# One decoder layer with a 32-expert mixture: how the first expert pair gets its rows, where LayerNorm's weights enter, and how head means are spread

## The chip, the cores and the metric

One core of one Trainium2 chip runs the whole layer as one program. The metric is device time in microseconds (us), the median of the runs shown. Engines: TensorE (PE; its weight loads are PEld), VectorE (DVE), ScalarE (ACT), GpSimd (POOL) and SyncE (SP), which here only starts DMA transfers.

## The reference, cut to what matters

288 rows of 1024 fp32 numbers (256 of a prompt, 32 of samples) go through one layer:

```python
proj = x @ w_in                     # q, k, v of two head groups, 8 heads x 64 each
o    = attention of both groups     # block-sparse (here one block) and dilated windows
o    = concat(RMSNorm_head(o_A) * gn_moba, RMSNorm_head(o_B) * gn_win)
hx   = LayerNorm(alpha * x + o @ w_out) * ln1_g + ln1_b
logits = hx @ w_router + b_router   # top 4 of 32, softmax over the four -> comb
for e in range(32):                 # f, the mixture
    gu   = hx @ w_gate_up[e] + b_gate_up[e]
    act  = min(gate, 7) * sigmoid(1.702 * min(gate, 7)) * (clip(up, -7, 7) + 1)
    f   += comb[:, e] * (act @ w_down[e] + b_down[e])
y    = LayerNorm(alpha * hx + f) * ln2_g + ln2_b
```

The outputs are y, and the new key and value rows of both groups. The expert weights are 403 MB of the 454 MB that are moved.

## The kernel before, in words

Everything is fp32, and each engine has one instruction stream written out by hand; engines wait on each other's semaphores. Rows are held in `hx` as three tiles: two of 128 prompt rows, and one of 32 sample rows (`TILES`, line 21).

**Projection and attention.** 29 slots (line 867 on PE, 1342 on ACT, 1637 on DVE), each with one projection product and whatever tables such as `SCORE`, `MIX` and `KEY` put in it. `mean_squares` (700) multiplies the squares of a pair of heads by `blk64`, so that each of 128 partitions gets its head's mean; four results of 256 columns each lie side by side in `msq`. In slot 19 `root_means` (1334) takes the roots of the first four, and `scale_out` (1594) inverts them and multiplies `outT`. `turn_samples(0)` (823) and `samp_place(0)` (1615) bring the samples' outputs in slot 20. Four other head pairs follow as two halves in slots 26 and 27.

**Output product, LayerNorm, router.** The order of tiles is samples, first, second (`ORDER`). For each tile DVE adds alpha * x (`raw_sum`, 1705), PE turns the raw sum (`turn_hx`, 896) and forms the logits from it, since ln1's weights are folded into the router; ACT normalises (`normalise`, 1383), DVE multiplies by ln1_g (`gain`, 1698), POOL adds ln1_b (`add_bias`, 642). DVE's `choose` (1743) takes the top four; `place_early` and `place_last` (920, 929) count rows per expert; `pick` is then a matrix of zeros and ones, rows by slots, 64 slots for each expert of a pair.

**Expert pairs.** Sixteen pairs. A pair's weights are 12 units of 2 MB: eight of gate_up, four of down. SP loads them into a ring of eight buffers (`load_unit`, 429; `unit_free`, 504). A unit is loaded over the one eight units before it, once PE has read that one. Unit 0 of the first pair has a buffer of its own, `first`, so the first pair's units 0 to 8 can be loaded ahead; units 9, 10, 11 of it and unit 0 of the second wait for its units 1, 2, 3, 4 to be read. PE's order for a pair is: `gather` (1026; pick times hx, 6 products), `turn_weights`, `turn_act`, `down` (1085) of the pair before with `turn_slots` (1035) of the new one in it, four bias products for each expert in `begin_gate_up` (1128), `gate_up` (1041) with `combine` of the pair before in it. The first pair instead forms its turned rows at once in `gather_first` (941), 24 products of 128 columns, and `add_biases` (1006) puts combT times b_down into the sums after unit 3. ACT copies turned rows to `xg` (1420).

Between unit 8 and units 9 on, SP has a wait of its own:

```python
        sp.wait_ge(S.hx_ready, 5)            # 495
        sp.wait_ge(S.hx_last, 1)
        sp.dma_start(ln_g[:, :], ln2_g[0:1, :].broadcast_to([128, D])).then_inc(S.ln2_in, 16)
```

Of the kernel before, what the change touches and what calls it, by code (L numbers as in the profile page):

```python
# [63 lines left out]
def constant_tables():  # L64
# [11 lines left out]
    att = np.zeros((128, A_END + 128), np.float32)  # L76
    att[:, A_END:] = (p[:, None] // HD == p[None, :] // HD) / HD
# [30 lines left out]
def build_layer(nc, x_prompt, x_sample, cache_k, cache_v, state_k, state_v, page_table, w_in, gn_moba,  # L108
# [9 lines left out]
    def place(name, shape, at=None, dt=F32):  # L118
# [44 lines left out]
    ln_gs, ln_bs = place("ln_gs", [128, 256]), place("ln_bs", [128, 256])  # L163

# [7 lines left out]
    blk64 = place("blk64", [128, 128], at=share_at + 2592)  # L172
# [7 lines left out]
    bdn = place("bdn", [E, D], at=ybuf_at)  # L180
    combT = place("combT", [E, T], at=spread_at)
# [15 lines left out]
    msq = place("msq", [128, 4, SEQ])  # L197
    upper = place("upper", [NS, 512], at=top_at + 4096)
# [10 lines left out]
        probs_copied head_mixed out_taken squared msq_done msq_taken msq_rooted outT_ready  # L209
# [3 lines left out]
        hx_ready hx_last hx_raw hx_halved hx_turned hxT_ready router_folded router_summed routed logits_read logits_used  # L213
# [5 lines left out]
        y_ready mixed added y_varied y_rooted y_scaled y_centred y_gained hx_gained y_normed y_done y_moments y_shared  # L219
        sums_whole copies_out  # L220
# [37 lines left out]
    c_folded, c_consts = columns(2 * E), columns(2 * E)  # L258
# [103 lines left out]
    def _(sp):  # L362
# [109 lines left out]
        sp.dma_start(ln_b[:, :], ln1_b[0:1, :].broadcast_to([128, D])).then_inc(S.ln1_in, 16)  # L472
# [10 lines left out]
        sp.dma_start(bdn[:, :], b_down[0]).then_inc(S.bdn_in, 16)  # L483
# [11 lines left out]
        sp.wait_ge(S.hx_ready, 5)  # L495
        sp.wait_ge(S.hx_last, 1)
        sp.dma_start(ln_g[:, :], ln2_g[0:1, :].broadcast_to([128, D])).then_inc(S.ln2_in, 16)
        sp.dma_start(ln_b[:, :], ln2_b[0:1, :].broadcast_to([128, D])).then_inc(S.ln2_in, 16)
# [28 lines left out]
        load_units(0, 0, range(9, UNITS))  # L527
        next_bias(0)
# [48 lines left out]
    def _(pool):  # L577
# [72 lines left out]
        pool.wait_ge(S.ln1_in, 32)  # L650
        for nth in range(2):
            add_bias(hx, ORDER[nth], S.hx_gained, S.hx_ready, nth)
        low = hx[:, ORDER[2], 0:512]
        pool.wait_ge(S.hx_centred, 5)
        nc.gpsimd.tensor_tensor(low, low, ln_g[:, 0:512], ALU.mult).then_inc(S.hx_halved, 1)
        pool.wait_ge(S.hx_halved, 1)
        nc.gpsimd.tensor_tensor(low, low, ln_b[:, 0:512], ALU.add).then_inc(S.hx_ready, 1)
        pool.wait_ge(S.ln2_in, 160)
# [1363 lines left out]
```

## Time and profile before

| | |
|---|---|
| median of 3 runs | 1183.83 us (1183.76 to 1184.81) |
| the profiled execution | 1188.98 us, its span 1187.1 us |
| instructions | 14412 |
| PE busy | 1141.0 us (96%) |
| DVE, ACT, POOL busy | 297.0, 175.3, 38.4 us |
| moved by DMA | 454.45 MB, mean 383 GB/s |
| mean granted clock of TensorE | 0.986 |

The span is the time from the first to the last instruction of the execution that was profiled. Times in the rows are microseconds from its start. A granted clock of 1.00 is 2.4 GHz, 0.50 is 1.2 GHz. In a line such as `144.36 0.41 PE L665 MATMUL ... x2 [3.38 <-DVE otS L1613]` the first number is the start, the second the time that the group takes, and the bracket is the idle time of the engine before it and what ended it. Matmuls overlap, so a busy PE need not be at its peak. A product of fp32 operands is two matmul instructions.

### The profile page before, as it was taken

To read this page: it belongs to the slowest core of one execution; us is meant where nothing else is said; L and a number is where in the kernel's file an instruction comes from. 1 tells how busy PE (TensorE), PEld (TensorE's weight loads), DVE (VectorE), ACT (ScalarE), POOL (GpSimd) and SP (SyncE) were. 2 spreads that over 40 slices of the span, in tenths; PEclk is the share of its full clock that TensorE was granted. 3 is DMA by queue.
4 is the path that set the end of the run, shared out by engine and by line. 5 is a ranking of instruction groups with operands and counts; after the bars stand their busy time and mean duration, and the time that the engine had idled before them with its cause. 6 is when DMAs were issued, how large, how long until landed. Compare 5 with 4: busy or idle time off the path is not lost.

```text
span 1187.1 us, 14412 instructions
## 1 busy us (share of the span) xinstructions
PE 1141.0 (96%) x5520; PEld 469.3 (40%) x5521; DVE 297.0 (25%) x702; ACT 175.3 (15%) x381; POOL 38.4 (3%) x71
## 2 busy tenths in 40 slices
PE   8999889999999999999999999999999999999996
PEld 6877654553333333333333333333333333333332
DVE  1453756822021212121211203030303030303113
ACT  1332322211010101010202010101010111111111
POOL 0110111200000000000000000000000000000001
PEclk9999999889999999999999999999999999999998
DMA  9957749758999999999999999999999999999993
GB/s 350 320 195 255 266 176 413 305 199 344 407 427 426 428 428 427 428 428 428 428 428 428 428 428 428 428 427 428 428 428 428 428 428 427 428 428 428 413 422 123
DMA packets 83397, 454.45 MB, mean 383 GB/s; under 512 B 7146, under 2 KB 20098, under 8 KB 36130
## 3 DMA queue, kind: packets, MB, share of 16 engines
q1 hardware_dynamic: 81008, 441.49, 90.2%
q0 software_dynamic: 1728, 10.75, 2.4%
q10 hardware_dynamic: 626, 1.75, 0.4%
q8 instruction: 21, 0.34, 0.1%
q14 instruction: 14, 0.11, 0.0%
HBM read 450.43 MB, written 11.93 MB: 389 GB/s over the span
## 4 chain that ended last, share of the span: by engine, by line
PE 75%; DMA 18%; DVE 4%; ACT 2%; SPq 1%; issue 1%; DVEq 0%
PE bank L1055 23%; PE bank L1097 18%; DMA ring<-in_w_gate_up 16%; PE bank L1031 8%; PE bank L688 6%; PE bank L665 5%; PE bank L1122 3%; PE bank L835 2%; PE bank L691 2%; DMA ring<-in_w_down 2%; PE bank L1206 1%; PE bank L790 1%; PE bank L1138 1%; PE bank L956 1%; SPq L448 1%; ACT actT L1286 1%
## 5 line engine op out<-in xcount | busy, mean ns | idle before, releaser
L1055 PE MATMUL bank<-ring,xg 128*64 128x512 f32 x1904 | 420.6, 598 | 10.6 <-DMA ring<-in_w_gate_up 10.6
L1055 PEld LDWEIGHTS bank<-ring,xg 128*64 128x64 f32 x1904 | 133.6, 137 | 288.9 <-issue 263.6
L1097 PE MATMUL bank<-ring,actT 128*64 128x512 f32 x960 | 215.9, 597 | 3.8 <-ACT actT L1286 3.8
L1888 DVE TENSOR_TENSOR acc<-acc,bank 128x512 f32<-128x512 f32 x60 | 41.2, 687 | 493.6 <-PE bank L1122 493.6
L1097 PEld LDWEIGHTS bank<-ring,actT 128*64 128x64 f32 x960 | 66.6, 137 | 121.5 <-issue 118.7
L1429 ACT ACTIVATE sig<-gate 128x256 f32<-128x256 f32 x64 | 26.7, 417 | 528.0 <-DVE gate L1870 528.0
L1031 PE MATMUL bank<-hx,pick 128*128 128x512 f32 x180 | 90.0, 625 | 0.0
L1870 DVE TENSOR_SCALAR gate<-bank 128x256 f32<-128x256 f32 x64 | 26.9, 420 | 186.7 <-PE bank L1055 166.5
L688 PE MATMUL bank<-xT,wblk 128*128 128x288 f32 x256 | 68.4, 423 | 0.9 <-DVE xT L1517 0.9
L1122 PE MATMUL bank<-ybuf,spread 128*128 128x512 f32 x120 | 58.4, 618 | 0.0
L688 PEld LDWEIGHTS bank<-xT,wblk 128*128 128x128 f32 x256 | 49.4, 198 | 16.4 <-issue 2.4
L1031 PEld LDWEIGHTS bank<-hx,pick 128*128 128x128 f32 x180 | 29.1, 187 | 60.7 <-issue 60.7
L1286 ACT ACTIVATE xg<-bank 128x512 f32<-128x512 f32 x32 | 19.1, 597 | 126.2 <-PE bank L665 112.0
L835 PE MATMUL bank<-wout,outT 128*128 128x512 f32 (+1 forms) x96 | 36.6, 600 | 0.4 <-ACT kstage L1286 0.4
L1122 PEld LDWEIGHTS bank<-ybuf,spread 128*128 128x128 f32 x120 | 19.1, 188 | 39.0 <-DVE acc L1888 19.7
L648 POOL TENSOR_TENSOR acc<-acc,ln_b 128x512 f32<-128x512 f32 x2 | 3.0, 1510 | 945.7 <-DVE acc L1981 945.7
L1286 ACT ACTIVATE ybuf<-bank 128x512 f32<-128x512 f32 x31 | 16.9, 594 | 108.5 <-PE bank L1097 96.5
L691 PE MATMUL bank<-wblk,xT 128*128 128x256 f32 x128 | 30.1, 390 | 0.0
L1176 PE MATMUL bank<-ring,xg 128*64 128x512 f32 x128 | 28.6, 596 | 0.9 <-DMA ring<-in_w_gate_up 0.8
L1874 DVE SCALAR_TENSOR_TENSOR up<-up,gate 128x256 f32<-128x256 f32 x64 | 27.2, 425 | 2.7
L1871 DVE TENSOR_SCALAR up<-bank 128x256 f32<-128x256 f32 x64 | 26.6, 416 | 0.0
L691 PEld LDWEIGHTS bank<-wblk,xT 128*128 128x128 f32 x128 | 24.6, 197 | 3.4 <-issue 0.2
(236 smaller groups left out, 724.1 us busy)
## 6 DMA issues: line engine op xcount, KB each, us to landing
ring<-in_w_gate_up SPq DMA_DIRECT2D x119, 2048.0 KB, 25.4
ring<-in_w_down SPq DMA_DIRECT2D x63, 2048.0 KB, 27.2
ring<-in_w_gate_up SPq DMA_DIRECT2D x16, 1024.0 KB, 18.7
wblk<-in_w_in SPq DMA_DIRECT2D x12, 1024.0 KB, 8.0
kring<-in_cache_k_moba SPq DMA_DIRECT2D x16, 256.0 KB, 5.0
vring<-in_cache_v_moba SPq DMA_DIRECT2D x16, 256.0 KB, 5.1
out<-in_state_k_win POOLq DMA_DIRECT2D x8, 512.0 KB, 4.8
out<-in_state_v_win POOLq DMA_DIRECT2D x8, 512.0 KB, 5.8
```

Of the source, the lines that this page charges most:

```text
L665: return nc.tensor.transpose(out, in_, ident[0:in_.shape[0], 0:in_.shape[0]])
L688: ins = nc.tensor.matmul(out[:, 0:T], w[:, k, 128 * c:128 * c + 128], xT[:, k, :], start=(k == 0), stop=(k == KC - 1))
L691: ins = nc.tensor.matmul(out[:, 0:256], xT[:, k, 128 * c:128 * c + 128], w[:, k, :], start=(k == 0), stop=(k == KC - 1))
L835: return nc.tensor.matmul(out_bank(t, half), outT[:, k, t0:t0 + rows], wout[:, k, 512 * half:512 * half + 512], start=(k == 0), stop=(k == ...
L1031: ins = nc.tensor.matmul(bank[6 + a][:, :], pick[0:rows, t, :], hx[0:rows, t, 512 * a:512 * a + 512], start=(t == 0), stop=(t == 2))
L1055: ins = nc.tensor.matmul(bank[n][64 * e:64 * e + 64, :], xg[:, k, 64 * e:64 * e + 64], w[:, 2048 * e + 512 * n:2048 * e + 512 * n + 512], ...
L1097: ins = nc.tensor.matmul(bank[4 + half][64 * e:64 * e + 64, :], actT[:, j, 64 * e:64 * e + 64], w[:, at:at + 512], start=(j == 0), stop=(j ...
L1122: ins = nc.tensor.matmul(bank[4 + half][:, :], spread[:, t0:t0 + rows], ybuf[:, 512 * half:512 * half + 512], start=True, stop=True)
L1176: ins = nc.tensor.matmul(bank[n][64 * e:64 * e + 64, :], xg[:, k, 64 * e:64 * e + 64], w[:, at:at + 512], start=False, stop=(k == KC - 1))
L1286: return nc.scalar.activation(out, in_, ACT.Copy, **kw)
L1874: V.scalar_tensor_tensor(up[:, c], up[:, c], 1.0, gate[:, c], ALU.add, ALU.mult).then_inc(S.dve_moe, 1)
L1888: V.tensor_tensor(o, o, new, ALU.add).then_inc(S.added, 1)
```

## The change

- The copy of a normalised row no longer has ln1_g and ln1_b in `hx`. They enter where turned rows are copied to `xg`: eight ACT instructions with a scale and a bias for each partition in place of two copies. The sums get alpha * ln1_g * hx from DVE (`scale_sums`), and alpha * ln1_b as a 33rd row of b_down against a row of alpha in combT. POOL's work on `hx`, and DVE's `gain` and `last_half`, are gone.
- The first pair is gathered like the others: pick times hx tile by tile, copied to `xtok`, turned, copied to `xg`.
- The samples' part of every gather is two 32-row parts of the array, one for each half of the columns; for this the samples' second half is copied to partitions 32 to 63 (`lower_half`), and `posm` too.
- Bias products of a pair: four with 128 columns of weights in place of eight with 64.
- Of the first four head pairs the means lie in 32 partitions each of one 256-column tile; they are inverted at once, and PE spreads them (`spread_means`) before DVE scales. The samples' turn of group 0 moves from slot 20 to 24, to another bank.
- `add_biases` is split in three parts, after units 4, 5 and 6 of the first pair; `keep_warm(1)` is one product whose result is not used; ln2_b is loaded where ln1_b was; ln2_g is loaded after `scale_sums`, between units of the ring.

```diff
+        def spread_means(pair):
+            pe.wait_ge(S.msq_inverted, 1)
+            pe.wait_ge(S.outT_ready, pair)
+            for c in range(2):
+                j = 2 * pair + c
+                ins = nc.tensor.matmul(bank[4][:, 256 * c:256 * c + 256], heads_of[:, 128 * j:128 * j + 128], msq[:, 0, :],
+                                       start=True, stop=True)
+            ins.then_inc(S.means_spread, 1)
...
-            if slot in (20, 27):
-                turn_samples(0 if slot == 20 else 1)
+            if slot in (20, 21):
+                spread_means(slot - 20)
+            if slot in (24, 27):
+                turn_samples(0 if slot == 24 else 1)
...
+        def invert_means():
+            dve.wait_ge(S.msq_rooted, 1)
+            V.reciprocal(msq[:, 0, :], msq[:, 0, :]).then_inc(S.msq_inverted, 1)
+
+        def scale_pair(pair):
+            dve.wait_ge(S.means_spread, pair + 1)
+            o = outT[:, 2 * pair:2 * pair + 2, 0:SEQ]
+            V.tensor_tensor(o, o, bank[4][:, :].rearrange("p (c q) -> p c q", c=2), ALU.mult).then_inc(S.outT_ready, 1)
...
             if slot == 19:
                 samp_squares(0)
-                scale_out(0, 0, 4)
+                invert_means()
                 samp_norm(0)
-            if slot == 20:
+            if slot in (20, 21):
+                scale_pair(slot - 20)
+            if slot == 24:
                 samp_place(0)
...
+        def gather_samples():
+            for a in range(2):
+                r = slice(NS * a, NS * a + NS)
+                nc.tensor.matmul(bank[6 + a][:, :], pick[r, 2, :], hx[r, 2, 512 * a:512 * a + 512], start=True, stop=False,
+                                 tile_position=(NS * a, 0))
+
+        def gather_tile(t, a):
+            return nc.tensor.matmul(bank[6 + a][:, :], pick[:, t, :], hx[:, t, 512 * a:512 * a + 512], start=False,
+                                    stop=(t == 1))
+
+        def gather_first():
+            pe.wait_ge(S.first_picked, 1)
+            pe.wait_ge(S.hx_low, 1)
+            gather_samples()
+            place_last()
+            pe.wait_ge(S.hx_centred, 4)
+            for a in range(2):
+                gather_tile(0, a)
+            pe.wait_ge(S.picked, 1)
+            for a in range(2):
+                pe.wait_ge(S.hx_centred, 5 + a)
+                gather_tile(1, a).then_inc(S.gathered, 1)
+
+        def keep_warm(n):
+            for _ in range(n):
+                nc.tensor.matmul(bank[0][:, :], ident, keep[:, 0:512], start=True, stop=True)
...
         turn_hx(2, 0)
         place_early()
+        keep_warm(1)
         turn_hx(2, 1)
...
         begin_gate_up(0)
-        place_last()
-        for nth in range(3):
-            gather_first(nth)
-        gate_up(0, 0, 0, {1: turn_comb, 3: add_biases})
+        place_known()
+        gather_first()
+        turn_slots(0, 0)
+        turn_slots(0, 1)
+        gate_up(0, 0, 0, {1: turn_comb, 4: lambda: add_biases(0), 5: lambda: add_biases(1), 6: add_sample_biases})
...
-                for e in range(2):
-                    ins = nc.tensor.matmul(bank[n][64 * e:64 * e + 64, :],
-                                           keep[r, C_SEL + SLOTS * e:C_SEL + SLOTS * (e + 1)],
-                                           bias_rows[r, :], start=True, stop=False, tile_position=(32 * n, 64 * e))
+                ins = nc.tensor.matmul(bank[n][:, :], keep[r, C_SEL:C_SEL + 2 * SLOTS], bias_rows[r, :], start=True,
+                                       stop=False, tile_position=(32 * n, 0))
...
-                copy(xg[:, 4 * a:4 * a + 4, :], bank[7 - a][:, :].rearrange("p (k s) -> p k s", k=4)).then_inc(S.xg_ready, 1)
+                for k in range(4 * a, 4 * a + 4):
+                    ins = nc.scalar.activation(xg[:, k, :], bank[7 - a][:, 128 * (k % 4):128 * (k % 4) + 128], ACT.Identity,
+                                               bias=s_(c_cols + KC + k), scale=s_(c_cols + k))
+                ins.then_inc(S.xg_ready, 1)
...
         load_units(0, 0, range(9, UNITS))
+        sp.wait_ge(S.sums_scaled, 6)
+        sp.dma_start(ln_g[:, :], ln2_g[0:1, :].broadcast_to([128, D])).then_inc(S.ln2_in, 16)
         next_bias(0)
```

## Rows read from the trace of the kernel before

**Rows 1.** The page: GB/s in 40 equal slices of the span.
```profile
GB/s 350 320 195 255 266 176 413 305 199 344 407 427 426 428 428 427 428 428 428 428 428 428 428 428 428 428 427 428 428 428 428 428 428 427 428 428 428 413 422 123
```
**Rows 2.** The chain that ended last: gathers of two early and two late pairs.
```profile
340.37 5.95 PE bank L1031 x12
...
397.15 5.95 PE bank L1031 x12
...
854.27 5.94 PE bank L1031 x12
...
877.92 31.79 DMA ring<-in_w_gate_up
...
913.41 5.94 PE bank L1031 x12
```
**Rows 3.** Stages: busy PE, PEld, DVE, ACT, POOL; granted clock; DMA share; GB/s.
```profile
255.00:310.00 55.00, 54.65 (x241) 18.32 (x239) 9.95 (x23) 7.93 (x15) 0.00 (x0) 0.94 0.90 360
360.00:1100.00 740.00, 724.13 (x3269) 245.54 (x3267) 128.84 (x299) 84.45 (x167) 0.00 (x0) 1.00 1.01 428
```
**Rows 4.** Timeline: PE's first pair, and SP's issues for the ring.
```profile
247.08 3.65 PE L1055 MATMUL bank<-first,xg 128*64 128x512 f32 x16 [0.69 <-ACT xg L1286]
...
254.21 7.84 SPq L438 DMA_DIRECT2D ring<-in_w_down  x3
...
273.44 34.14 SPq L438 DMA_DIRECT2D ring<-in_w_gate_up  x8
...
295.33 0.66 PE L665 MATMUL bank<-keep,xtok 128*128 128x128 f32 x4
```
**Rows 5.** Timeline of DVE, then of PE, in slots 19 to 21.
```profile
136.09 6.55 DVE L1597 RECIPROCAL msq<-msq 128x1024 f32<-128x1024 f32 x1 [1.28 <-ACT msq L1336]
142.68 1.23 DVE L1598 TENSOR_TENSOR outT<-outT,msq 128x1024 f32<-128x1024 f32 x1
...
149.64 0.95 DVE L1621 COPY outT<-bank 64x64 f32<-64x64 f32 x4
...
144.36 0.41 PE L665 MATMUL bank<-keep,otS 128*64 128x128 f32 x2 [3.38 <-DVE otS L1613]
144.60 3.62 PE L691 MATMUL bank<-wblk,xT 128*128 128x256 f32 x16
...
148.93 0.66 PE L665 MATMUL bank<-keep,kring 128*128 128x128 f32 x4 [0.27 <-DVE kT L1560]
152.77 0.55 PE L665 MATMUL bank<-keep,sampP 128*128 128x128 f32 x3 [3.19 <-DVE sampP L1566]
```
**Rows 6.** Stages as in rows 3, with PE at the lower clock.
```profile
153.00:157.00 4.00, 4.00 (x16) 3.49 (x15) 1.21 (x3) 1.02 (x3) 0.00 (x0) 0.57 0.00 0
...
229.00:245.00 16.00, 16.00 (x82) 13.78 (x83) 5.85 (x23) 2.17 (x4) 2.53 (x2) 0.50 0.70 262
...
266.00:272.00 6.00, 6.00 (x24) 1.56 (x18) 1.02 (x3) 0.00 (x0) 0.00 (x0) 0.50 0.86 362
```
**Rows 7.** Timeline of PE from the logits of the first tile on.
```profile
218.63 1.87 PE L914 MATMUL bank<-wrt,outT 128*128 128x32 f32 x16
...
227.07 0.40 PE L925 MATMUL bank<-mask,keep 32*128 32x32 f32 x2 [2.63 <-DVE mask L1757]
...
228.72 3.46 PE L914 MATMUL bank<-wrt,outT 128*128 128x32 f32 x16
232.11 2.01 PE L1138 MATMUL bank<-bias_rows,keep 2*64 2x512 f32 x16
...
236.33 10.06 PE L956 MATMUL bank<-pick,hx 32*128 32x128 f32 x48
...
307.10 1.11 PE L1138 MATMUL bank<-bias_rows,keep 2*64 2x512 f32 x16
```
**Rows 8.** POOL's second addition, and one DVE line: min/median/max ns of three.
```profile
223.40 2.87 POOL L648 TENSOR_TENSOR hx<-hx,ln_b 128x512 f32<-128x512 f32 x2 [3.91 <-DVE hx L1703]
...
L1754 DVE CAST small<-idx_u x3: 172/1020/1031, 218.5 to 233.8; 128x8 f32<-128x8 uint32 x3
```

More of the change, by code:

```diff
@@ L494, in _ @@
             load_unit(0, 0, u)
[L495 to L498, printed above, removed]
+        sp.wait_ge(S.hx_raw, 2)
         for q in range(4):
@@ L936, in place_last @@
                 nc.tensor.matmul(at, ones[:, 0:rows], first_tile, start=False, stop=False)
+        def place_last():
+            out = bank[5]
             pe.wait_ge(S.masks_ready, 3)
@@ L1004, in turn_comb, with add_biases, add_sample_biases @@
             ins.then_inc(S.comb_turned, 1)
-        def add_biases():
-            pe.wait_ge(S.combT_ready, 1)
-            pe.wait_ge(S.bdn_in, 16)
-            for j in range(4):
-                t, half = divmod(j, 2)
-                t0, rows = TILES[t]
-                if j >= 2:
-                    pe.wait_ge(S.added, j - 1)
-                nc.tensor.matmul(bank[4 + half][0:rows, :], combT[:, t0:t0 + rows],
+        def add_biases(t):
+            t0 = TILES[t][0]
+            for half in range(2):
+                if t == 0 and half == 0:
+                    pe.wait_ge(S.combT_ready, 1)
+                    pe.wait_ge(S.bdn_in, 32)
+                if t == 1:
+                    pe.wait_ge(S.added, half + 1)
+                nc.tensor.matmul(bank[4 + half][:, :], combT[:, t0:t0 + 128],
                                  bdn[:, 512 * half:512 * half + 512], start=True, stop=True).then_inc(S.spread_down, 1)
+        def add_sample_biases():
             pe.wait_ge(S.added, 3)
+            pe.wait_ge(S.sums_scaled, 2)
             for q in range(4):
                 r, c = slice(NS * q, NS * q + NS), slice(256 * q, 256 * q + 256)
-                nc.tensor.matmul(bank[4][r, 0:256], ident[0:NS, 0:NS], hx[0:NS, 2, c], start=True, stop=True,
+                nc.tensor.matmul(bank[4][r, 0:256], ident[0:NS, 0:NS], samp_x[:, c], start=True, stop=True,
                                  tile_position=(0, NS * q))
@@ L1028, in gather @@
             pe.wait_ge(S.actT_ready, turned_before)
+            gather_samples()
             for a in range(2):
-                for t, (t0, rows) in enumerate(TILES):
-                    ins = nc.tensor.matmul(bank[6 + a][:, :], pick[0:rows, t, :], hx[0:rows, t, 512 * a:512 * a + 512],
-                                           start=(t == 0), stop=(t == 2))
-                ins.then_inc(S.gathered, 1)
+                gather_tile(0, a)
+                gather_tile(1, a).then_inc(S.gathered, 1)
         def turn_slots(i, a):
@@ L1832, in _ @@
         moments(2, 0)
-        gain(hx, ORDER[1], 1, S.hx_centred, S.hx_gained)
+        lower_half()
         choose(1)
@@ L1904, in _ @@
         weigh_slots(0, 0)
+        scale_sums()
         pick_slots(1, 1, 0)
```

155 lines of the change are left out of this document (71 added, 84 removed).

## Prediction

> **What bounds the kernel now.** I read the page's DMA line first. The reader is to see that from about 300 us on the transfers run at 427 or 428 GB/s to the end, and that the holes lie before that [rows 1]. The stage of 740 us says it with a share: 1.01 at 428 GB/s, and PE busy beside it [rows 3]. So both look full; the chain tells which counts. An early pair takes 397.15 - 340.37 = 56.8 us from gather to gather, on PE; a late pair 913.41 - 854.27 = 59.1 us, and half of that is a wait for gate_up weights [rows 2]. PE is the faster one by 2.3 us a pair and runs into the transfers at last. The ring is then refilled without a hole, so the end is this: the moment when the stream of weights starts for good, plus the bytes left over 428 GB/s, plus a tail that the change leaves alone. What PE saves inside a pair of the loop is worth nothing; what lets the stream start earlier, or fills a hole in it, is worth all of it.
>
> The stream starts when PE has read unit 1 of the first pair: PE begins at 247.08, SP issues at 254.21 [rows 4], 7.1 us later. Then a hole: units 9, 10, 11 go out, and the next waits for unit 4, which comes after add_biases: 273.44 [rows 4]. In 255 to 310 the rate is 360 GB/s [rows 3]: 55 x (1 - 360/428) = 8.7 us of transfer are missing, 0.5 of it the lag of the first issue, so 8.2 us of hole.
>
> Three things to work out, then: how much earlier PE begins the first pair (A, B), how much of the hole goes (C), and what is new in the transfers (D). The sum is made in the profiled execution (1188.98 us, span 1187.1), and the difference is taken off the median, 1183.83, which is 5.2 us (0.4%) below it.
>
> **A. Head means and the samples' turn.** DVE inverts 1024 columns in 6.55 us and multiplies in 1.23; PE stands 3.38 us for the samples behind it, 0.27 for a copy and 3.19 for the probabilities sampP, in all 6.84 us [rows 5]. In 153 to 157 the granted clock is then 0.57 [rows 6]: 4 x 0.43 = 1.7 us more. After: 256 columns, 6.55/4 = 1.64 us; the multiplication and the samples' copies (0.95) move behind. DVE reaches sampP earlier by 4.9 + 1.2 + 0.95, less a scaling of about 0.7 (half of 1.23 and PSUM's read), some 6.4 us: 152.7 becomes 146.3. PE without waits gets there at 152.77 - 6.84 + 0.9 = 146.8. So DVE is just in time; what is late next is PE's own row of projections. PE gains two times four products of 256 columns at 3.62/16 = 0.23 us: 1.8 us. A = -6.84 - 1.7 + 1.8 = -6.7. If half of the waits return as another wait of the same slots, and the clock falls after it all the same, A = -1.6. Behind it transfers stood still (0 GB/s in 153 to 157 [rows 6]), so all loads up to unit 8 can move with PE.
>
> **B. From the router to the first pair.** PE waits 2.63 us for the second tile's mask [rows 7]. DVE's chain to it loses two multiplications by ln1_g (1.3 us each in other rows of that form) and the delays beside POOL: the cast takes 1020 ns in the median where the third took 172, and POOL's additions lie over both of the long casts (one of them shown) [rows 8]. That is over 3 us in each of two chains, so the 2.63 go. keep_warm adds 2 products of 512 columns, 0.9 us.
> From 227 on nearly all of PE's work ran at clock 0.50 [rows 6]: logits 3.46 against 1.87 before, bias products 2.01 against 1.11 later, the gather 10.06 [rows 7]. What is there after, at clock 1.00, from 224.45: place 0.9, keep_warm 0.9, turn 0.6, ACT's copy 0.6 and half the logits 0.9, bias 1.0, six small count products 1.2, samples 1.0, four tile products 3.5, ACT's copy 0.6, two turns 1.5, ACT's last four 128-column copies 1.0, semaphores 0.3: 14.0, the first pair at 238.4, 8.6 us earlier. (Items without a row here are read from the same timeline, halved where it ran at 0.50. 512 columns at 1.00: the loop's gather, 5.95 us for 12 [rows 2], of which the four with few rows take longer, so 0.43 for the others.) At clock 0.50 from the logits on, 8.2 us of these double: 246.6, 0.5 us earlier. So B lies between -8.6 and -0.5. I take the middle, -4.6: keep_warm stands right where the clock fell, but after it come two or three us of small products, of few rows and few columns, which is what ran when it fell before; and the full-width gather is then the sort of work in which it came back.
> Cost at nothing: lower_half (about 0.4 us of DVE), hidden by DVE's wait for the second tile's logits; scale_sums (4 products of 0.69 and two more, done about 8 us after the picks), hidden, since SP's new wait for it stands behind unit 11, 14 us after PE begins; behind that wait are the next pair's biases and all of its units. Uncovered, each us late is a us of hole. Eight ACT copies in the loop: PE asks for xg a whole half of down() later.
>
> **C. The hole.** From unit 1 read to unit 8 read PE took 295.33 - 254.21 = 41.1 us [rows 4]. Seven units of 2.097 MB at 428 GB/s are 34.3 us, and ln2_g is 1.2 us in the same stream: 35.5. PE's way gets shorter by the gather (5.95 to 4.7), by 3.0 us if the spell at 0.50 in 266 to 272 [rows 6] goes, by 0.5 for the biases' waits: 36.4, and 0.9 of hole is left; with the spell, 3.9. I take 2.3, and 0.7 for unit 9: hole 8.2 to 3.0. With ln2_g's bytes C = -5.2 + 1.2 = -4.0 (from -6.1 to -1.5).
>
> **D. New bytes.** 0.28 MB of tables at the start, where DMA is the limit: 0.65 us at 428 GB/s; half of it lies beside PE's turning: +0.3 (0 to 0.7).
>
> **The loop.** The gather loses its second small-row pass, 1.2 us a pair; bias products 0 to 0.5. PE's pair: 55.6 or less against 59.1. Worth 0 while transfers bound.
>
> Where the trace and a page could part: the four small-row products cost 5.95 - 8 x 0.43 = 2.5 us, 0.6 each, more than a full-row one. The Trainium skill (TensorEngine Tiling (Array Packing), Tiling Modes, Key Properties) says that going from one tiling of the array to another drains the engine, which speaks against 32-row parts between full tiles. By the row, the switches are paid for already and become fewer; by the page alone each pair would pay two drains, and the sum here stays as it is, since it is within PE's 3.5 us of slack.
>
> **Sum.** -6.7 - 4.6 - 4.0 + 0.3 = -15.0: span 1172.1, median 1168.8. All at their best: -6.7 - 8.6 - 6.1 = -21.4, 1162.4. All at their worst: -1.6 - 0.5 - 1.5 + 0.7 = -2.9, 1180.9.
>
> **Rivals.** (1) The clock stays low: 0.50 from the logits to well into the first pair, and again at its biases. For it: it was 0.50 through 16 us in which PE was busy all the time [rows 6], and the new order has as many small products there. Against: keep_warm, and 512 columns in place of 128. A stays, B -0.5, C -1.5, D +0.3: -8.4, 1175.4. The Trainium skill (TensorE: Matmul & The Clock Gate, Part 1) calls the low clock the default, which activity lifts; this trace agrees in that it fell behind the 2.63 us of waiting [rows 6, 7]; by the page alone the new order, without that wait, should keep the clock, as in B's better end. (2) A's waits come back as others (DVE has only 0.5 us to spare at sampP): A -1.6, the rest as forecast, -9.9, 1173.9. (3) Everything is hidden by transfers, which would need a stream that has no hole before 300 us; [rows 1] shows several: 0, 1183.8. (4) Slower: the gather's small-row parts and its turns bring the clock down inside every pair. Such a spell costs 3 us (6 us at 0.50 [rows 6]). One a pair gives 58.6 and is hidden; from two on PE passes 59.1: 61.6, 15 x 2.5 = 37.5 lost, 15 won: 1206. Against: the old gather had small-row products too, and the clock stayed at 1.00 through 740 us [rows 3]. (5) The 32-row parts do not run side by side: 0.9 us in B, nothing in the loop: 1169.7.
>
> **Chances.** Forecast with (5), -12 to -21: 0.65. (1) 0.17. (2) 0.10. (3) 0.04. (4) 0.04. The range 1161.5 to 1177.5 leaves out (3), (4) and combinations of (1) with (2). No change is within 0.2%, 2.4 us, about what a measurement of this kernel can tell: same 0.04, slower 0.04, faster 0.92.
>
> **What would show it.** A: the samples' scores of slot 20 and the second turn of slot 21 on PE with under 1 us between, no bracket at sampP, clock 1.00 through, projection of slot 22 near 149. B: no wait at the mask line; first unit near 236 (before: 247.08), 232 at clock 1.00 and 240 at 0.50. C: the rate between SP's first issue of unit 9 and 50 us later near 400 GB/s, no pause in issues after unit 11. Loop: 59.1 us a pair from the second or third pair on, PE waiting at gate_up, 428 GB/s. Wrong if a late pair is not bound by transfers, or if PE begins the first pair at the same place.

## The result, and the profile after

Measured: 1180.58 us (1178.47 to 1182.39, 15 runs), against 1185.14 (1183.76 to 1189.3) for the kernel before in the same runs, 4.6 us less by the medians. The ratio of the runs, which is not the quotient of the two medians, is 0.995, interval [0.994, 0.996], so 4.7 to 7.1 us less. The forecast was 1168.8, with a range of 1161.5 to 1177.5. The sign was right, the size wrong by 11.8 us, and the time lies outside the range. The profiled execution of after took 1180.89 us.

The page after: the rates in 40 equal slices.
```profile
GB/s 361 324 197 254 269 270 384 257 263 341 423 428 427 427 428 428 429 428 428 428 428 428 428 428 428 428 427 428 429 428 428 428 428 428 428 428 428 413 424 108
```
The span is 1178.8 us, 8.3 us shorter than in the first profile (1187.1), and the picture is that of [rows 1]: holes until about 300 us, then 427 to 429 GB/s. What has to be compared is again how early the stream of weights starts for good.

Timeline of after in slots 20 to 22 (DVE's inversion, then PE; a bracket would be idle time ahead of the row). It answers to [rows 5].
```profile
135.28 1.75 DVE L1636 RECIPROCAL msq<-msq 128x256 f32<-128x256 f32 x1 [0.64 <-ACT msq L1364]
...
141.71 3.62 PE L690 MATMUL bank<-wblk,xT 128*128 128x256 f32 x16
...
146.04 0.49 PE L664 MATMUL bank<-keep,sampP 128*128 128x128 f32 x3
...
147.89 3.62 PE L690 MATMUL bank<-wblk,xT 128*128 128x256 f32 x16
```
No bracket is left; the projection of slot 22 starts at 147.89 and takes 3.62 us, which is clock 1.00.

Timeline of PE in after, from the logits to the first pair, answering to [rows 7] and the first row of [rows 4]:
```profile
217.67 1.10 PE L987 MATMUL bank<-keep 128*128 128x512 f32 x2
...
219.04 1.93 PE L932 MATMUL bank<-wrt,outT 128*128 128x32 f32 x16
...
222.79 1.70 PE L964 MATMUL bank<-hx,pick 32*128 32x512 f32 x4
...
225.12 6.12 PE L968 MATMUL bank<-hx,pick 128*128 128x512 f32 x8
231.92 1.09 PE L664 MATMUL bank<-keep,xtok 128*128 128x128 f32 x8 [0.69 <-ACT xtok L1313]
235.57 5.35 PE L1083 MATMUL bank<-first,xg 128*64 128x512 f32 x16 [2.56 <-ACT xg L1450]
240.75 3.60 PE L1083 MATMUL bank<-ring,xg 128*64 128x512 f32 x16
```
The first pair starts at 235.57 (before 247.08). The logits ran at full speed, the four gather tiles did not (x8, since each product is two instructions): later in this trace they take 3.70 us, here 6.12. And the first unit took 5.35 us where the second took 3.60.

Stages of after: busy PE, PEld, DVE, ACT, POOL; granted clock; DMA share; GB/s. They answer to [rows 3, 6].
```profile
224.00:230.00 6.00, 6.00 (x12) 2.79 (x11) 4.32 (x17) 0.00 (x0) 0.00 (x0) 0.50 0.90 351
...
236.00:241.00 5.00, 5.00 (x18) 1.55 (x16) 0.00 (x0) 0.00 (x0) 0.00 (x0) 0.66 0.00 0
...
270.00:275.00 5.00, 5.00 (x17) 1.58 (x18) 3.06 (x8) 0.83 (x2) 0.00 (x0) 0.66 1.01 426
...
255.00:310.00 55.00, 54.50 (x229) 18.39 (x229) 10.04 (x23) 8.35 (x19) 0.00 (x0) 0.97 0.92 374
360.00:1100.00 740.00, 708.96 (x3161) 244.06 (x3159) 128.67 (x299) 107.42 (x245) 0.00 (x0) 1.00 1.01 428
```
Three spells at 0.50 (1.2 GHz) are left: some 7 us before the first pair, and two of about 3.4 us inside it. From 360 to 1100 nothing is new but PE's busy time, 15 us less.

Timeline of SP's issues for the ring in after (and PE's turn before unit 8 is free), answering to [rows 4]:
```profile
244.40 7.84 SPq L445 DMA_DIRECT2D ring<-in_w_down  x3
...
255.30 43.24 SPq L445 DMA_DIRECT2D ring<-in_w_gate_up  x8
...
286.29 0.66 PE L664 MATMUL bank<-keep,xtok 128*128 128x128 f32 x4
```
The start of the stream comes 9.8 us earlier than in the first profile. But from unit 9's issue to the freeing of unit 8 PE takes 286.29 - 244.40 = 41.9 us. It was 41.1, and 36.4 were forecast. In place of a stretch that shrinks there is one that grew a little.

Where the 5.5 us of that stretch are, the samples' bias products show. First the kernel before, the products on `hx` and on `bdn`, then the next unit (engine, line, rows*columns of the weights, the moving operand):
```profile
265.38 0.74 PE L1020 MATMUL bank<-hx,keep 32*32 32x256 f32 x8
265.84 1.13 PE L1022 MATMUL bank<-bdn,combT 32*32 32x256 f32 x8
266.90 5.39 PE L1055 MATMUL bank<-ring,xg 128*64 128x512 f32 x12
```
The same in after:
```profile
266.18 0.61 PE L1049 MATMUL bank<-samp_x,keep 32*32 32x256 f32 x2
266.73 0.62 PE L1051 MATMUL bank<-bdn,combT 33*32 33x256 f32 x2
...
270.54 2.43 PE L1083 MATMUL bank<-ring,xg 128*64 128x512 f32 x6
```
Before, all eight products take 266.90 - 265.38 = 1.5 us; after, one starts every 0.545 us, 270.54 - 266.18 = 4.4 us. The change gave `combT` and `bdn` a 33rd row (`33*32`), and it is a product of that kind that now alternates with one of 32 rows. Then the clock falls (0.66 in 270 to 275).

### The profile page after: what moved, and what is told of

It is laid out like the page before. It is cut to its first block, busy times and chain, and to the rows that moved or that the text cites. A ratio compares the mean times of both kernels' runs of the same rounds, so it can differ in the third digit from the quotient of the medians.

```text
span 1178.8 us, 14219 instructions
## 1 busy us (share of the span) xinstructions
PE 1121.9 (95%) x5374; PEld 457.7 (39%) x5375; DVE 289.7 (25%) x707; ACT 203.8 (17%) x479; POOL 30.1 (3%) x65
## 4 chain that ended last, share of the span: by engine, by line
PE 65%; DMA 26%; SPq 5%; ACT 2%; DVE 1%; issue 1%
DMA ring<-in_w_gate_up 23%; PE bank L1083 19%; PE bank L1125 15%; PE bank L968 5%; PE bank L664 5%; PE bank L687 5%; SPq L445 3%; PE bank L851 3%; PE bank L690 2%; DMA ring<-in_w_down 2%; PE bank L1150 2%; PE bank L964 1%; SPq L455 1%; PE bank L804 1%; ACT xtok L1313 1%; ACT actT L1313 1%
## 5 line engine op out<-in xcount | busy, mean ns | idle before, releaser
L1450 ACT ACTIVATE xg<-bank,small 128x128 f32<-128x128 f32 x128 | 48.1, 458 | 99.1 <-PE bank L664 99.1
L968 PE MATMUL bank<-hx,pick 128*128 128x512 f32 x128 | 61.6, 626 | 0.0
L968 PEld LDWEIGHTS bank<-hx,pick 128*128 128x128 f32 x128 | 24.0, 197 | 35.8 <-issue 35.8
L1921 DVE TENSOR_TENSOR up<-up,sig 128x256 f32<-128x256 f32 x64 | 25.3, 417 | 0.0
```

What stands on the lines that cost most here:

```text
L968: return nc.tensor.matmul(bank[6 + a][:, :], pick[:, t, :], hx[:, t, 512 * a:512 * a + 512], start=False, stop=(t == 1))
L1450: ins = nc.scalar.activation(xg[:, k, :], bank[7 - a][:, 128 * (k % 4):128 * (k % 4) + 128], ACT.Identity, bias=s_(c_cols + KC + k), scale ...
```

## The experiments

Times are medians; each ratio is against the kernel before in the same set of runs, whose own median moved from 1185.14 to 1187.27 between the sets. The four columns behind are read from one profiled execution, whose own time is given, since it can lie 3 us from the median. The last is the time from the issue of unit 9 until unit 8 is read and free.

| kernel | us | ratio to before | profiled us | first pair | unit 9 | unit 9 to unit 8 free |
|---|---|---|---|---|---|---|
| before, first profile | 1185.14 | 1 | 1188.98 | 247.08 | 254.21 | 41.1 |
| after | 1180.58 | 0.995 [0.994, 0.996] | 1180.89 | 235.57 | 244.40 | 41.9 |
| head means alone | 1181.21 | 0.9954 [0.994, 0.9967] | 1181.61 | 239.39 | 246.52 | 41.1 |
| samples' products grouped | 1174.44 | 0.9899 [0.9886, 0.9913] | 1171.77 | 232.13 | 240.75 | 37.0 |
| filling products | 1177.59 | 0.9936 [0.992, 0.9952] | 1175.3 | 233.85 | 240.97 | 40.2 |
| 3 products more a pair | 1188.2 | 1.0014 [1.0003, 1.0024] | 1189.92 | 235.52 | 244.35 | 43.5 |
| before again (one run) | 1185.87 |  | 1185.87 | 243.25 | 250.38 | 41.1 |
| grouped, filled, copy shared | 1171.95 | 0.9874 [0.9856, 0.9892] | 1172.15 | 233.44 | 240.57 | 37.0 |
| no warming product | 1179.11 | 0.9941 [0.9926, 0.9955] | 1178.33 | 233.26 | 242.08 | 41.8 |
| loop's gather as before | 1181.66 | 0.9962 [0.9949, 0.9976] | 1181.14 | 233.89 | 242.72 | 44.7 |
| samples' products, 32 rows | 1174.93 | 0.9902 [0.9882, 0.9922] | 1174.69 | 235.51 | 244.33 | 36.9 |
| as the best, no warming | 1174.15 | 0.989 [0.9868, 0.9911] | 1174.52 | 235.02 | 242.15 | 37.0 |
| grouped, copy shared | 1173.68 | 0.9883 [0.9858, 0.9909] | 1174.64 | 235.93 | 243.06 | 37.0 |

**The head means alone**, put into the kernel before; the router, the gather and the pair are as they were. In words:
```diff
-    spread head means with blk64 (128x128), 1024 columns inverted
+    means of each pair of heads in 32 partitions of one tile, 256 columns inverted, spread by heads_of after it
+    samples' turn in slot 24
```


> The kernel before with the head means alone (means in 32 partitions each, one inversion of 256 columns, PE spreads them, the samples' turn moved to slot 24). Theory (the stream's start sets the end): PE stops waiting in slots 20 and 21, reaches the first pair 6.5 to 7.5 us earlier, SP issues unit 9 as much earlier, and the hole behind it stays: 6 to 7 us less than the kernel before, ratio 0.994 to 0.995. That would be as much as the whole change gives. Rival (what is won in attention is hidden by transfers or taken by a later wait): under 2 us.

PE's timeline at the mask and the first pair, and SP's issue of unit 9, in this kernel:
```profile
219.89 0.63 PE L949 MATMUL bank<-mask,keep 32*128 32x32 f32 x2 [2.64 <-DVE mask L1797]
...
239.39 3.65 PE L1079 MATMUL bank<-first,xg 128*64 128x512 f32 x16 [0.69 <-ACT xg L1310]
...
246.52 7.84 SPq L443 DMA_DIRECT2D ring<-in_w_down  x3
```
1181.21 us: this one part wins what the whole change wins (0.9954 against 0.995, intervals over each other). It is 4.9 us less than its own kernel before (1186.09), a little under the 6 to 7 expected; the interval of the ratio, 3.9 to 7.1 us, holds them. The first pair starts 7.7 us earlier than in the first profile. The wait at the mask is still there, 2.64 us. The whole change starts the pair 3.8 us earlier still and issues unit 9 2.1 us earlier, and has nothing to show for it: something in the pair takes it back.

**The samples' products in two groups.** Same products, other order.
```diff
             for q in range(4):
                 matmul(bank[4][r, 0:256], ident, samp_x[:, c], tile_position=(0, NS * q))
+            for q in range(4):
                 matmul(bank[4][r, 256:512], combT[:, SEQ:T], bdn[:, c], tile_position=(0, NS * q))
```


> The changed kernel, the samples' eight products of add_sample_biases in another order: first the four with the 32-row identity, then the four with the 33 rows of combT, in place of turn about. Theory: turn about, each product waits for the one before (0.55 us each, 4.4 us together, where the old kernel needed 1.6); in two groups they take about 1.8 us, the stretch from unit 1 read to unit 8 read shrinks from 41.9 to about 39, and the hole in the transfers with it: 2 to 4 us less than the changed kernel (1180.6), more if the clock no longer falls in the last unit. Rival (the 4.4 us come from the 33 rows themselves, or the hole is set by something else): no change, 1180.6.

Timeline of this kernel: SP's unit 9, the samples' products on PE, the unit behind them, the turn before unit 8 is free.
```profile
240.75 7.84 SPq L445 DMA_DIRECT2D ring<-in_w_down  x3
...
262.53 0.63 PE L1049 MATMUL bank<-samp_x,keep 32*32 32x256 f32 x8
263.09 0.64 PE L1053 MATMUL bank<-bdn,combT 33*32 33x256 f32 x8
263.66 3.65 PE L1085 MATMUL bank<-ring,xg 128*64 128x512 f32 x16
...
277.71 0.66 PE L664 MATMUL bank<-keep,xtok 128*128 128x128 f32 x4
```
The eight take 263.66 - 262.53 = 1.1 us, the unit behind them runs at full clock (3.65 us, where after took 5.35), and the stretch is 277.71 - 240.75 = 37.0 us. The time falls by 6.1 us. The profiled execution, 1171.77 us, was the shortest of the five, and not all that it shows is the order: in it the gather ran at clock 1.00 and the pair began at 232.13, before the changed place is reached. So the order was tested once more in another way, below.

How far the clock in the gather differs between executions, two profiles show. Up to the end of the first gather this kernel and the one with grouped products and shared copy (last in the table) give PE the same instructions. The window 224 to 230 in this one, then in that one (the three last columns are clock, DMA share, GB/s):
```profile
224.00:230.00 6.00, 4.88 (x18) 2.38 (x18) 5.35 (x19) 2.03 (x5) 0.00 (x0) 1.00 0.84 336
...
224.00:230.00 6.00, 6.00 (x13) 2.46 (x10) 3.32 (x15) 0.00 (x0) 0.00 (x0) 0.50 0.86 340
```
Of eight traces with the same instructions there (the after kernel's and those of seven experiments), this one shows no fall of the clock before the first pair; in the others it fell between 221.7 and 224.4. In the five of them that also turn and copy as the after kernel does, the first pair begins between 232.13 and 235.57. So a difference of up to 3.4 us in the table's column for the first pair can be that of two executions and not of two kernels.

**Filling products**, one of 512 columns before the turned rows and three behind them, on a bank that is free there.
```diff
         gather_first()
+        keep_warm(1, 4)
         turn_slots(0, 0)
         turn_slots(0, 1)
+        keep_warm(3, 4)
```


> The changed kernel with one full product whose result is not used between the first pair's gather and its turns, and three after the turns, so that PE works where it stood 0.7 and 2.6 us. Theory: the clock stays at 1.00 in the first pair's first unit (it was 0.50 for 3.4 us, 1.7 us of loss), unit 9 is issued 1 to 1.7 us earlier, total 1 to 2 us less than the changed kernel. Rival (the clock falls there for another reason, or the fillers delay the first pair as much as they win): 0 to 0.5 us more.

1177.59 us; six runs from 1175.3 to 1181.26, so the interval is wide, and the profiled execution is the shortest of them. It shows the first unit at 3.65 us in place of 5.35, and unit 9 3.4 us earlier (240.97). PE no longer stands idle while ACT copies, and the spell in the first unit is gone; that is 1.7 of the 3.4 us, and the rest is there before the first filling product, in a shorter spell in the gather. The samples' eight products alternate as in after and take 267.12 - 262.76 = 4.4 us, but the unit behind them runs at full clock:
```profile
267.12 3.65 PE L1083 MATMUL bank<-ring,xg 128*64 128x512 f32 x16
```
The stretch is 40.2 us, and the hole behind unit 11 stays:
```profile
275.00:285.00 10.00, 9.50 (x49) 3.86 (x47) 0.56 (x1) 3.49 (x8) 0.00 (x0) 1.00 0.64 248
```
248 GB/s over 10 us: an earlier start does not mend C.

**Three products more in each pair of the loop** (2.6 us a pair, 14 pairs), to test the statement that PE's time in a pair is worth nothing.
```diff
-    gate_up(i + 1, ..., {3: lambda: combine(i)})
+    gate_up(i + 1, ..., {3: lambda: combine(i), 6: lambda: keep_warm(3, 7)})
```


> The changed kernel with three full products whose results are not used after unit 6 of gate_up in each of 14 pairs of the loop: 2.6 us of PE a pair, 36 us in all. Theory (from about 300 us on only transfers count, PE has 3.5 us a pair to spare): no change, within 1 us of 1180.6. Rival (PE's chain through the pairs is part of the end): up to 36 us more; half of the pairs PE-bound would give some 18.

The loop's stage in this kernel, and then the gathers of an early and of a late pair on PE's timeline:
```profile
360.00:1100.00 740.00, 733.42 (x3196) 255.07 (x3193) 128.29 (x298) 102.34 (x233) 0.00 (x0) 1.00 1.01 428
```
```profile
336.84 3.70 PE L968 MATMUL bank<-hx,pick 128*128 128x512 f32 x8
395.32 3.70 PE L968 MATMUL bank<-hx,pick 128*128 128x512 f32 x8
...
921.18 3.70 PE L968 MATMUL bank<-hx,pick 128*128 128x512 f32 x8
979.65 3.70 PE L968 MATMUL bank<-hx,pick 128*128 128x512 f32 x8
```
And in after:
```profile
332.35 3.70 PE L968 MATMUL bank<-hx,pick 128*128 128x512 f32 x8
387.90 3.70 PE L968 MATMUL bank<-hx,pick 128*128 128x512 f32 x8
...
728.24 3.70 PE L968 MATMUL bank<-hx,pick 128*128 128x512 f32 x8
787.38 3.70 PE L968 MATMUL bank<-hx,pick 128*128 128x512 f32 x8
```
7.6 us slower than after, where no change was expected, although the transfers' mean rate is 428 GB/s from 360 to 1100 in both. The added work takes PE's pair from 55.5 to 58.4 us, early and late, so PE enters the stage behind the stream and never catches up: at 921 it still goes at its own pace. In after it goes at 55.55 us until about 610 and is held by the transfers (59.14) from then on: in five or six pairs it caught up 59.14 - 55.55 = 3.6 us each, a lag of 18 to 22 us. Fifteen pairs give PE 54 us of slack, the lag takes its part, 32 to 36 are left, and 14 x 2.9 = 41 do not fit: 5 to 9 us too much, 7.6 measured. This sum is an estimate; what the traces show beside it is that behind 300 us PE waits for weights 27.1 us in all in after and not once here. "Worth nothing" holds up to a sum over the loop, not for each pair by itself.

**The kernel before once more**, unchanged, for its profile.

> The kernel before, unchanged, profiled a second time. Its first profiled execution took 1188.98 us, where the median of its other executions is 1185 to 1186. Theory (the prediction read its terms from an execution in which the clock fell at costlier places than usual): here the stretch from SP's issue of unit 9 to PE's last turn before unit 8 is read, 41.1 us in the first profile, is shorter by the 3 us of the spell at 0.50 behind add_biases, and the time is near 1185. Rival (the same spells in every execution, the 4 us are overhead of the profiler): again near 1189 with the spell at the same place.

Its logits of the first tile, its first pair, SP's unit 9, and the turn before unit 8 is free:
```profile
215.33 1.87 PE L914 MATMUL bank<-wrt,outT 128*128 128x32 f32 x16
...
243.25 3.65 PE L1055 MATMUL bank<-first,xg 128*64 128x512 f32 x16 [0.69 <-ACT xg L1286]
...
250.38 7.84 SPq L438 DMA_DIRECT2D ring<-in_w_down  x3
...
291.43 0.66 PE L665 MATMUL bank<-keep,xtok 128*128 128x128 f32 x4
```
Span 1184.1 us in place of 1187.1. The stretch is 291.43 - 250.38 = 41.05 us, the same as in the first profile, against what was expected of it. The 3 us lie ahead: the logits start at 215.33 (218.63 in [rows 7]). 1.6 us of it are there before the scores of slot 20, 1.7 come between them and those of slot 22: the wait at sampP is 0.98 us here in place of 3.19, and the clock fell ahead of it (0.63 in 143 to 150) and not behind it (1.00 in 150 to 157). The first profile was one of the longer executions (1188.98 us; the kernel's runs go from 1183.76 to 1189.3).

**Three things at once**: the grouped products, one filling product before and one behind the turned rows, and half of the first `xg` copied by VectorE beside ScalarE. Of the edit only the third is shown:
```diff
-        take_slots(0)
+        take_slots(0, (0,))                       # ACT: the first half
+        for k in range(4, KC):                    # DVE: the second
+            V.tensor_scalar(xg[:, k, :], bank[6][...], s_(c_cols + k), s_(c_cols + KC + k), mult, add)
```


> The changed kernel with three edits: the samples' bias products in two groups (e2), one filler product before and one behind the first pair's turns, and the second half of the first xg copied by DVE beside ACT. Theory (the end is the start of the stream of weights plus what hole is left): PE begins the first pair 1 to 1.5 us earlier than in e2 and at clock 1.00 more often, no hole: 2 to 3 us below e2, 1171.5 to 1172.5. Rival (with the hole gone the transfers are bound by something earlier, such as the loading of units 7 and 8): as e2, 1174.4.

The first pair on its timeline, and then the stage behind (the last column is GB/s):
```profile
233.44 3.65 PE L1085 MATMUL bank<-first,xg 128*64 128x512 f32 x16 [1.21 <-DVE xg L1954]
```
```profile
245.00:310.00 65.00, 64.50 (x293) 21.79 (x291) 13.51 (x29) 8.35 (x19) 0.00 (x0) 1.00 1.00 410
```
1171.95 us, the best of all: 0.9874 of before, 0.7% ahead of after (1171.95 / 1180.58 = 0.9927; the two were not timed in the same runs, but their ratios, 0.9874 and 0.995, say the same). Against after its unit 9 is 3.8 us earlier and its stretch 4.9 us shorter; 8.7 in all, and the span is 8.6 shorter (1170.2).

**Without the warming product** (`keep_warm(1)` between the turned rows and the last logits), all else as after.
```diff
-        keep_warm(1)
```


> The changed kernel without keep_warm(1), the one product behind the router's counting. Theory A (it keeps the clock up at least through the logits): without it the clock falls one spell earlier, as in the kernel before, and it costs 1 to 3 us. Theory B (the clock falls behind it in any case, when the small products of the counts and biases run): 0.9 us is won or nothing, 1179.7 to 1180.6.

1179.11 against 1180.58: 1.5 us less, about the product's own 0.95 us, but the intervals of the ratios lie over each other. In the profile the clock falls all the same, at about 223.5, and the first unit takes 5.35 us again. The product wins nothing here that a run shows.

**The loop's gather as before**: six full-width products a pair in place of the two-part samples and four tiles.
```diff
-            gather_samples()
             for a in range(2):
-                gather_tile(0, a)
-                gather_tile(1, a)
+                for t, (t0, rows) in enumerate(TILES):
+                    matmul(bank[6 + a], pick[0:rows, t, :], hx[0:rows, t, ...])
```


> The changed kernel with the loop's gather as before: six products, the samples' part one full-width product for each half of the columns, not two 32-row parts. Theory: PE takes 1.2 us more a pair; 14 of the 15 are hidden by PE's room, one lies in the hole before unit 8 is read: 1.2 us more, 1181.8. Rival (the row parts count in every pair): up to 18 us more. Second rival (nothing at all): 1180.6.

1181.66, 1.1 us more than after: the 1.2 us of one gather (6.00 against 1.13 + 3.70), the one of the first pair, which lies in the stretch. (In its profile the stretch is 44.7 and not 43.1, because the unit ahead of the gather ran at the lower clock for longer, 6.49 us for it against 5.35.) That the other 14 cost nothing agrees with the loop's slack. The interval [0.9949, 0.9976] lies over after's, so the size is weakly shown.

**Alternating, but of 32 rows.** The order is after's; only the 33rd row is taken from the samples' `combT` products.
```diff
-                matmul(bank[4][r, 256:512], combT[:, SEQ:T], bdn[:, c], tile_position=(0, NS * q))
+                matmul(bank[4][r, 256:512], combT[0:NS, SEQ:T], bdn[0:NS, c], tile_position=(0, NS * q))
```


> The kernel after, in which the samples' four combT products read 32 rows (combT[0:32], bdn[0:32]) in place of 33; the order (samp_x and combT products in turn) is the kernel after's own. The 33rd row of comb is left out for the 32 sample rows, so their output lacks that row's part. Theory A (the 0.55 us each is paid because a product of 33 rows and one of 32 rows put TensorE's array into different row parts, and each change waits for the product before): the eight now take 1.2 us or less in all, as the two grouped runs of four did, and the time falls by what 3.2 us earlier at that place is worth: 1177.0 to 1178.5 us. Theory B (it is the alternation itself that costs: another moving operand, the other half of the bank, the column part that repeats): they take 4.4 us as before, and the time stays at 1180.6.

SP's unit 9, the samples' products, the unit behind them, and the turn before unit 8 is free; then the window in which after's clock was 0.66:
```profile
244.33 7.84 SPq L445 DMA_DIRECT2D ring<-in_w_down  x3
...
266.12 0.65 PE L1049 MATMUL bank<-samp_x,keep 32*32 32x256 f32 x8
266.57 0.63 PE L1051 MATMUL bank<-bdn,combT 32*32 32x256 f32 x8
267.13 3.65 PE L1083 MATMUL bank<-ring,xg 128*64 128x512 f32 x16
...
281.18 0.66 PE L664 MATMUL bank<-keep,xtok 128*128 128x128 f32 x4
```
```profile
270.00:275.00 5.00, 5.00 (x16) 1.85 (x13) 4.23 (x12) 1.83 (x4) 0.00 (x0) 1.00 1.02 433
```
This is the clean comparison. Unit 9 goes out where it does in after (244.33, 244.40). The eight take 267.13 - 266.12 = 1.0 us, alternating as they do; so it is the mix of 33 and 32 rows that costs, and neither the order as such nor the bank. The spell behind them is gone too, and the stretch is 36.9 us, half a us from the 36.4 forecast. The time is 1174.93: 5.65 us less than after (5.7 by the two ratios, 0.9902 and 0.995). 3.3 us of it are the products themselves and 1.7 the spell; 0.6 stays unexplained. That was more than the 2.1 to 3.6 us expected.

Whether the spell belongs to the alternation is not shown. In four of the five traces with it the unit behind took 4.98 to 6.54 us, but with the filling products 3.65. In the five traces with the products grouped or at 32 rows the clock stays up there. But in all three traces with before's bias products, which mix no 33rd row, it falls somewhere in 257 to 272.

**The best version without the warming product.**
```diff
-        keep_warm(1)
```


> The version of e6_fast_first (samples' products in two groups, one 128x512 product on bank 4 before and after the turned slots, half of the first xg copied by VectorE) without the warming product of L987 between the turned rows and the last logits. If that product only costs (as in the kernel after without it, -1.5 us): 1170.5 to 1171.5, against 1171.95. If in this version the clock falls earlier or longer without it: 1173 or more, and the first pair starts later than 230.2 us.

1174.15, the pair at 235.02 in place of 233.44: the clock was down from 221 on, where in the version with the product it fell at 224. The first expectation was 0.5 to 1.5 us less; the time is in the second's, 1173 or more. (The 230.2 us of the expectation is no sign: it is where the turned rows begin in the version with the product, whose pair begins at 233.44.) But the early fall is not the missing product's for certain: in the next kernel, which has it, the clock fell at 221.7. And the ratios 0.989 [0.9868, 0.9911] and 0.9874 [0.9856, 0.9892] lie over each other, and the two were not timed in the same runs. Whether the product helps beside the fillers stays open.

**Grouped products and the shared copy, no filling.**

> The samples' products in two groups and half of the first xg copied by VectorE, without the two filling products. Against the grouped version alone (1174.4 us) the copy should be worth 1.0 to 1.4 us of the start (ScalarE's eight took 2.9 us, two engines with four each 1.5): 1173.0 to 1173.5. If it is the filling products that made the 2.5 us between the grouped version and the one with all three (1171.95), the time stays at 1174.4 and the clock reads 0.50 at the start of the first unit.

1173.68, 0.2 above its forecast, but the interval [0.9858, 0.9909] holds the grouped version's 0.9899. The trace shows the copy's worth: 1.46 us of waiting ahead of the first pair, where ACT alone made it 2.56. The first unit then ran at full clock, without filling products. The clock had fallen at 221.7 and stayed at 0.50 through the gather, so the pair begins at 235.93 all the same.

## Why the prediction was wrong in size

**What held.** That only the start of the stream and its holes count: in after unit 9 goes out 6.0 us earlier than in the repeated profile of before, the stretch behind it is 0.9 us longer, together -5.1, and the spans differ by -5.3 (1178.8, 1184.1). In the best version the same sum gave 8.7 for 8.6. Over all traces it reads so: from the moment when unit 8 is free to the end of the span it is 891.4 to 893.5 us in twelve of them, though that moment moves from 277.5 to 295.3. Only the kernel with three products more a pair takes longer, 900.0. What also held is the direction, and "no wait at the mask".

**A, -6.7 forecast.** From the head scores' first product of slot 20 (136.88 before, 136.71 after) to that of slot 22 the first profile of before takes 22.2 us and after 14.7: -7.4. Against the repeated profile (20.5) it is -5.8. DVE reached sampP in time, the clock kept up. A alone gave 1181.21, 4.9 us less than its own kernel before. Right.

**B, -4.6 forecast.** The first pair is 11.5 us earlier than in the first profile; without A's 7.4, -3.9 (upstream 0.2 off). The spell at 0.50 came, in the middle between B's two ends, as taken: 224 to 230 and not the logits. Right, but by a choice between bounds and not by a mechanism, and with luck: over the five traces that turn and copy in the same way the same reckoning gives -3.9 to -7.3. Two sizes were off: ACT's eight copies took 2.91 us, 0.36 from one to the next in place of 0.25, and the spell inside the first unit (236 to 241, after 2.56 us of waiting for the copies) adds 1.7 us between the pair's start and unit 9. The working took the 7.1 us between the two as fixed; it was 8.8.

**C, -4.0 forecast: the step that failed.** "PE's way gets shorter by the gather (5.95 to 4.7), by 3.0 us if the spell at 0.50 in 266 to 272 [rows 6] goes, by 0.5 for the biases' waits: 36.4"; the sum then took half of the spell. The gather did get shorter (1.13 + 3.70). The term for the biases was mis-sized: it counted a wait that goes and not what the products become. They went from 1.5 us to 4.4, +2.8 in place of -0.5, and the spell stayed (1.7 us in 270 to 275). With the samples' products at 32 rows the stretch is 36.9 and the kernel at 1174.93. That term, with the spell that went in the same run, is 5.65 of the 11.8 us; the products by themselves are 3.3. The 33rd row of `bdn` and `combT` was in the description of the change, and the working gave it no price.

The Trainium skill (TensorEngine Tiling (Array Packing), Tiling Modes, Key Properties) has the rule that going from one tiling mode to another drains the engine, and lists 32-row and 64-row parts as different modes. The prediction weighed it for the gather alone, where PE's slack hides it. For the eight products the traces agree with it, if a product of 33 rows is taken to need a 64-row part; no row of a profile names the mode. They also say what it costs: in two groups, one mode change between them, 1.1 us for eight (0.57 us for four in four column parts side by side); in alternation 0.545 us for each. So the price of a change is not a fixed time on top (two groups cost 0.1 us more than none): in alternation the four column parts no longer run beside each other, and each product costs what a group of four does.

**D and the loop.** D (+0.3) can't be told apart. "Worth 0 while transfers bound" was true of what the change saves and wrong as a rule: 2.6 us more a pair cost 7.6.

**Slips in the working.** C's worst end is -2.4 by its own terms (a hole of 3.9 + 0.7), not -1.5. "Half of that is a wait for gate_up weights" is the share of the chain that ended last, not PE's idle time: the page of before has 10.6 us of waiting for gate_up weights ahead of all of gate_up's products together. In A, "PE gains" 1.8 us means that it has 1.8 us more to do, as the sum has it.

**The base.** The sum was made against one execution, 1188.98 us, 3.8 above the kernel's median, whose repeat has a span 3.0 us shorter; and it was taken off 1183.83, the median of three runs, where fifteen give 1185.14. So the 11.8 us come apart like this. Between the two profiled executions the gain is 1188.98 - 1180.89 = 8.1 in place of 15.0: 6.9 us, which are the samples' products with their spell (5.65) and the spell in the first unit (1.7), less 0.4 that other terms did better (the 5.65 is a difference of medians, the others are read from single profiles, so this split is good to about 1 us). The profiled execution of before lay 3.8 above its median, that of after 0.3: 3.5 us. And the median moved by 1.3.

**The rivals.** (1), the clock stays low, 1175.4, holds a part: 0.50 before the pair, in its first unit and behind the biases. It came out too low since it left the stretch without the added 2.8 us. (5), the 32-row parts do not run side by side, named the mechanism, but for the first gather, at 0.9 us, not for the samples' products inside the hole. (2), (3) and (4) did not come: no wait is left in slots 20 and 21, and the clock is 1.00 through the loop. The chance of 0.65 for the forecast was too high for a sum of four terms with no bound for one of its products.

## What to carry to other kernels

When a diff adds one row to an operand, look at each product that reads it and has only a small part of the array: here products of 32 rows in four column parts ran beside each other, 33 next to 32 one after another, four times as long, and grouping them got it back without changing the arithmetic. Where an end is set by a stream of transfers, read the stretch between the first issue and the next buffer that comes free, product by product; every us of it is a hole. Take a second profile of the kernel before ahead of a sum of waits: two executions of it differed by 3.1 us, about half of it in the slots whose waits were to be removed. And take more than one of the kernel after before reading a start from it.

## What the runs showed that was not expected

- A product of 33 rows and 256 moving columns in a 32-column part costs 0.545 us alternating with one of 32 rows, and 0.14 us (0.57 for four) in a group of its kind. Behind the alternation the clock fell in after (0.66 in 270 to 275) and not with 32 rows at the same place and time; but with the filling products it did not fall behind the same alternation either.
- The clock fell in after at 223.2 with PE busy throughout, no bracket standing at any of its rows since 213. The Trainium skill (TensorE: Matmul & The Clock Gate, Part 1) has the low clock as the default and activity as what lifts it; by busy time alone this trace does not agree, in which PE was busy all through the fall. What ran before the fall were the logits and then products of few rows or few columns (220.9 to 222.8). With the same instructions it did not fall at all in the trace of the grouped products, and fell at 221.7 in that of the grouped products with the shared copy.
- ScalarE's copy of 128x128 from PSUM with scale and bias took 0.45 to 0.49 us by itself and 0.36 from one to the next in a row, its plain copy of 128x512 0.60: eight small ones (2.91 us) cost more than twice what the same 1024 columns do in two (1.20).
